# A recurrence pipeline in another order: inverse, state and output work of a chunked scan re-sequenced on PE, VectorE and ScalarE

## The reference

```python
def _wkv_step(S, inp):
    r_t, w_t, k_t, v_t, a_t, b_t = inp
    sa = jnp.einsum('zbhvk,zbhk->zbhv', S, a_t)
    S = S * w_t[..., None, :] + sa[..., :, None] * b_t[..., None, :] + v_t[..., :, None] * k_t[..., None, :]
    return S, jnp.einsum('zbhvk,zbhk->zbhv', S, r_t)

def rwkv_out(y, h, xx, r, k_mod, v, mu, ln_g, ln_b, r_k, g1, g2, wo):
    ...
    y = layernorm(y, ln_g.reshape(RWKV_HEADS, RWKV_HEAD), ln_b.reshape(RWKV_HEADS, RWKV_HEAD), GN_EPS)
    bonus = jnp.einsum('bthk,zbthk->bth', _heads(r) * r_k, _heads(k_mod))
    y = y.astype(r.dtype) + bonus[..., None] * _heads(v)
```

## Time and profile before

| | us |
|---|---|
| median of 3 runs (lowest, highest) | 3682.07 (3679.72, 3685.00) |
| profiled execution, its own time | 3685.94 |
| its span, first to last instruction | 3684.0 |
| granted TensorE clock, mean over the span | 0.863 |
| PE busy, share of the span | 2950.9, 80% |
| VectorE (DVE) busy | 1179.1, 32% |
| ScalarE (ACT) busy | 484.1, 13% |
| GpSimd (POOL) busy | 241.5, 7% |
| the scan, from 2377.5 to 3002.1 of the span | 624.6 |

### The profile page before, as it was taken

One profiled execution on the slowest core, in us unless ns is written; L12 is line 12 of the kernel. 1 busy time (PEld: TensorE's weight loads), 2 busy tenths in 40 slices (PEclk: granted clock), 3 DMA queues, 4 the chain that ended last, 5 costly groups with the idle time before them and its releaser, 6 DMA issues. The chain is left out here.

```text
span 3684.0 us, 58651 instructions
## 1 busy us (share of the span) xinstructions
PE 2950.9 (80%) x25609; PEld 2059.6 (56%) x25609; DVE 1179.1 (32%) x2475; ACT 484.1 (13%) x1017; POOL 241.5 (7%) x230
## 2 busy tenths in 40 slices
PE   6999859999799897487777469788888883878775
PEld 5877625787684553344444224377777862444443
DVE  3562374355115102310000142265565522100002
ACT  1000212100111000100000000143333311000001
POOL 0000000000000000100000000032222201000000
PEclk9999755999699678599898779899999996998997
DMA  6774110577123100699999701000000016999994
GB/s 216 240 222 129 42 63 1 199 243 231 46 74 98 34 23 11 258 384 396 398 395 391 274 31 62 23 3 3 3 3 3 3 47 264 388 392 395 394 392 195
DMA packets 288698, 642.12 MB, mean 174 GB/s; under 512 B 27625, under 2 KB 180761, under 8 KB 254921
## 3 DMA queue, kind: packets, MB, share of 16 engines
q1 hardware_dynamic: 243124, 540.54, 40.1%
q10 hardware_dynamic: 37910, 74.88, 5.6%
q0 software_dynamic: 7424, 23.12, 2.1%
HBM read 611.70 MB, written 26.77 MB: 173 GB/s over the span
## 5 line engine op out<-in xcount | busy, mean ns | idle before, releaser
L1624 PE MATMUL bank<-expert_weights,ex_xt 128*64 128x256 f32 x2688 | 346.5, 417 | 100.3 <-DMA expert_weights<-in_moe_w_up_dram 100.0
L1624 PEld LDWEIGHTS bank<-expert_weights,ex_xt 128*64 128x64 f32 x2688 | 233.1, 151 | 228.0 <-issue 158.0
L444 PE MATMUL bank<-u,weights 128*128 128x272 f32 (+1 forms) x1408 | 318.6, 390 | 14.0 <-DVEq L465 14.0
L444 PEld LDWEIGHTS bank<-u,weights 128*128 128x128 f32 x1408 | 270.7, 192 | 62.0 <-DVEq L465 14.8
L1675 DVE TENSOR_TENSOR ex_hidden<-ex_silu,bank 128x256 f32<-128x256 f32 x64 | 26.9, 421 | 716.1 <-ACT ex_silu L1660 716.1
L1624 PE MATMUL bank<-weights,ex_xt 128*64 128x256 f32 x1408 | 186.7, 426 | 53.0 <-DMA weights<-in_moe_w_up_dram 51.5
L1032 DVE SCALAR_TENSOR_TENSOR ada_acc<-ada_w,cond,ada_acc 128x512 f32 (+1 forms) x336 | 227.5, 744 | 0.0
L515 PE MATMUL bank<-rw_mixed,weights 128*128 128x512 f32 (+2 forms) x448 | 188.5, 582 | 39.7 <-DVEq L523 36.2
L1624 PEld LDWEIGHTS bank<-weights,ex_xt 128*64 128x64 f32 x1408 | 124.2, 154 | 122.1 <-issue 85.9
L515 PE MATMUL bank<-hidden,weights 128*128 128x272 f32 (+1 forms) x704 | 160.8, 392 | 14.9 <-DVEq L523 14.9
L1645 PE MATMUL bank<-expert_weights,ex_hidden_turned 128*64 128x512 f32 x672 | 153.5, 598 | 21.7 <-DVE ex_hidden_turned L1678 21.7
(11 more groups left out here) (503 smaller groups left out, 4311.6 us busy)
## 6 DMA issues: line engine op xcount, KB each, us to landing
expert_weights<-in_moe_w_gate_dram SPq DMA_DIRECT2D x84, 1024.0 KB, 26.1
expert_weights<-in_moe_w_up_dram SPq DMA_DIRECT2D x84, 1024.0 KB, 26.6
expert_weights<-in_moe_w_down_dram SPq DMA_DIRECT2D x84, 1024.0 KB, 26.0
ada_w<-in_ada_w_dram ACTq DMA_DIRECT2D x24, 2048.0 KB, 8.7
weights<-in_moe_w_gate_dram SPq DMA_DIRECT2D x44, 1024.0 KB, 25.4
weights<-in_moe_w_up_dram SPq DMA_DIRECT2D x44, 1024.0 KB, 26.0
weights<-in_moe_w_down_dram SPq DMA_DIRECT2D x44, 1024.0 KB, 25.8
weights<-in_w_gate_dram SPq DMA_DIRECT2D x22, 1024.0 KB, 5.3
```

The costliest lines, as they stand in the source:

```text
L444: last = nc.tensor.matmul(k.bank[b + side * NB][:, 0:N], w[:, f, c * P:(c + 1) * P], rhs[:, f, 0:N], start=(f == DC - 1), stop=(f == 0))
L1624: last = nc.tensor.matmul(half_cols(k.bank[2 + side], t), xt[:, s, f * SLOTS:(f + 1) * SLOTS], w[:, q * 512 + t * 256:q * 512 + t * 256 + ...
```

## The change

Which piece follows which in the three loops is changed, four methods are split so that their parts can stand at different places, and three waits are adapted. No instruction's shape changes and no arithmetic.

- PE: in the tail of a pass the level-5 t of direction 1, and side product 0 of the *next* back half, come ahead of the last xt; the first y sum follows them. The second y sum moves into the next pass, between side products 1 and 2. The next pass begins with n of direction 0; t(1,0) comes ahead of side product 6 and of decay.
- VectorE: `dve_out` is split in three: one instruction after t(1,0), two between rs(0) and xt(1,0), four between update(0) and the decay scan. The exponents are split in one and two instructions. The root moves ahead of xt(4,0). t(5,1) and the second operands move ahead of spread, and `dve_mean` goes to the next pass.
- ScalarE: `act_powers` is split. Square and bonus copy stay at the end of level 3; the first Exp follows update(6), the second x(4,1), the third with the small ones the end of level 4. The copy of side product 0 moves to the tail, the y square and y root to the next pass.
- Unchanged is who empties what: xt of direction 0 stays with VectorE.
- Waits: the first operands wait for `powered` after the second Exp, and only their last instruction (rt) for the rest; side product 0 waits for a new semaphore `bonus_kept`, raised by the bonus copy.

The loops, cut to what the prediction speaks of:

```diff
     def pe(self, pe):
-            if back:
-                self.pe_side(pe, b, 0)
-                self.pe_side(pe, b, 1)
             if front:
                 self.pe_n(pe, c, 0)
             if back:
+                self.pe_side(pe, b, 1)
+                self.pe_y_sum(pe, b - 1, self.q.fix, self.y_squared)
                 self.pe_side(pe, b, 2)
-                self.pe_side(pe, b, 3)
             if front:
                 self.pe_n(pe, c, 1)
             if back:
-                for n in range(4, 7):
+                for n in range(3, 6):
                     self.pe_side(pe, b, n)
+            if front:
+                self.pe_t(pe, c, 1, 0)
+            if back:
+                self.pe_side(pe, b, 6)
             if following:
                 self.pe_decay(pe, p)
-            if front:
-                self.pe_t(pe, c, 1, 0)
...
             if front:
                 self.pe_xt(pe, c, LEVELS - 1, 0)
+                self.pe_t(pe, c, LEVELS - 1, 1)
+                self.pe_side(pe, c, 0)
+                self.pe_xt(pe, c, LEVELS - 1, 1)
             if back:
                 self.pe_y_sum(pe, b, self.q.y, self.y_copied)
-            if front:
-                self.pe_t(pe, c, LEVELS - 1, 1)
-                self.pe_xt(pe, c, LEVELS - 1, 1)
-            if back:
-                self.pe_y_sum(pe, b, self.q.fix, self.y_squared)
+        self.pe_y_sum(pe, DC - 1, self.q.fix, self.y_squared)
...
     def dve(self, dve):
-            if ended:
-                self.dve_out(dve, c - 2)
             if front:
                 self.dve_t(dve, c, 1, 0)
+            if ended:
+                self.dve_out_root(dve, c - 2)
...
                 if back:
                     self.dve_rs(dve, b, i)
+                if ended and level == 1:
+                    self.dve_out_scale(dve, c - 2)
+                if following and level == 4:
+                    self.dve_root(dve, p)
                 if front:
                     self.dve_xt(dve, c, level)
...
                 if back:
                     self.dve_update(dve, b, i)
+                if ended and level == 1:
+                    self.dve_out_gate(dve, c - 2)
                 if following and level == 1:
                     self.dve_decay(dve, p, 0)
...
+                if following and level == 3:
+                    self.dve_exponents(dve, p, 0)
                 if front:
                     self.dve_t(dve, c, level + 1, 0)
...
     def act(self, act):
+                if following and level == 4:
+                    self.act_power(act, p, 0)
                 if back:
                     self.act_rs(act, b, i + 1)
                 if front:
                     self.act_x(act, c, level, 1)
+                if following and level == 4:
+                    self.act_power(act, p, 1)
                 if back:
                     self.act_sa(act, b, i + 1)
...
                 if following and level == 3:
-                    self.act_powers(act, p)
+                    self.act_bonus(act, p)
+            if following:
+                self.act_power(act, p, 2)
...
     def dve_operands(self, dve, c, z):
         if z == 0:
-            dve.wait_ge(self.powered, 2 * c + 2)
+            dve.wait_ge(self.powered, 2 * c + 1)
...
+        if z == 0:
+            dve.wait_ge(self.powered, 2 * c + 2)
         nc.vector.tensor_tensor(rt[:, z, :], q.r[:, c, :], q.G[:, z, :], ALU.mult).then_inc(self.rt_made, 1)
```

More of the change, by code:

```diff
@@ L2467, in dve @@
             b, p = c - 1, c + 1
+            if front:
+                self.dve_n(dve, c, 0)
             if back:
                 self.dve_side(dve, b, 1)
-            if front:
-                self.dve_n(dve, c, 0)
+            if ended:
+                self.dve_mean(dve, c - 2)
             if back:
@@ L2504, in dve @@
                 if following and level == 3:
-                    self.dve_exponents(dve, p)
-                if following and level == 4:
-                    self.dve_root(dve, p)
+                    self.dve_exponents(dve, p, 1)
                 if back:
@@ L2517, in dve @@
                     self.dve_side(dve, b, 8)
-                if following and level == 4:
-                    self.dve_operands(dve, p, 0)
+            if following:
+                self.dve_operands(dve, p, 0)
             if front:
                 self.dve_xt(dve, c, LEVELS - 1)
+                self.dve_t(dve, c, LEVELS - 1, 1)
             if back:
                 self.dve_center(dve, b)
-            if front:
-                self.dve_t(dve, c, LEVELS - 1, 1)
-            if back:
-                self.dve_spread(dve, b)
             if following:
@@ L2668, in dve_mean, with dve_out_root, dve_out_scale @@
             .then_inc(self.m_made, 1)
-    def dve_out(self, dve, b):
+    def dve_out_root(self, dve, b):
+        q, link = self.q, self.link
+        dve.wait_ge(self.y_rooted, 3 * b + 3)
+        link(self.nc.vector.scalar_tensor_tensor(out=q.fix[:, :], in0=q.fix[:, :], scalar=-0.5, in1=q.m[:, :],
+                                                 op0=ALU.mult, op1=ALU.mult))
+    def dve_out_scale(self, dve, b):
         nc, q, link = self.nc, self.q, self.link
-        dve.wait_ge(self.y_rooted, 3 * b + 3)
-        link(nc.vector.scalar_tensor_tensor(out=q.fix[:, :], in0=q.fix[:, :], scalar=-0.5, in1=q.m[:, :],
-                                            op0=ALU.mult, op1=ALU.mult))
         link(nc.vector.scalar_tensor_tensor(out=q.fix[:, :], in0=q.fix[:, :], scalar=1.5, in1=q.root[:, :],
@@ L2691, in act @@
             if back:
-                self.act_side(act, b, 0)
-                for n in range(3, 7):
+                self.act_y_square(act, b - 1)
+                self.act_side(act, b, 3)
+                self.act_y_root(act, b - 1)
+                for n in range(4, 7):
                     self.act_side(act, b, n)
@@ L2713, in act @@
                 if front:
-                    self.act_xt(act, c, level)
+                    self.act_xt(act, c, level, 1)
                 if back and i + 1 < self.LAST:
@@ L2766, in act_powers, with act_power @@
         after(act, self.y_done, p - 2)
-        nc.scalar.activation(q.bonus[p % 3][:, :], k.bank[4][:, 0:SEQ], ACT.Copy)
-        act.wait_ge(self.scaled, p + 1)
-        after(act, self.rt_made, 2 * p)
-        nc.scalar.activation(q.Gp[:, :, :], q.Gp[:, :, :], ACT.Exp, scale=DECAY)
-        nc.scalar.activation(q.lg[:, :, :], q.F[:, :, :], ACT.Exp, scale=-DECAY).then_inc(self.powered, 1)
-        nc.scalar.activation(q.G[:, :, :], q.F[:, :, :], ACT.Exp, scale=DECAY)
-        for z in range(2):
-            after(act, self.s_kept[z], 7 * (p - 2))
-            edge = q.F[:, z, CH - 1::CH] if z == 0 else q.F[:, z, 0::CH]
-            last = nc.scalar.activation(q.pend[p % 3][:, z, :], edge, ACT.Exp, scale=DECAY)
-        last.then_inc(self.powered, 1)
+        nc.scalar.activation(q.bonus[p % 3][:, :], k.bank[4][:, 0:SEQ], ACT.Copy).then_inc(self.bonus_kept, 1)
+    def act_power(self, act, p, part):
+        nc, q = self.nc, self.q
+        if part == 0:
+            act.wait_ge(self.scaled, p + 1)
+            nc.scalar.activation(q.Gp[:, :, :], q.Gp[:, :, :], ACT.Exp, scale=DECAY)
+        elif part == 1:
+            nc.scalar.activation(q.lg[:, :, :], q.F[:, :, :], ACT.Exp, scale=-DECAY).then_inc(self.powered, 1)
+        else:
+            after(act, self.rt_made, 2 * p)
+            nc.scalar.activation(q.G[:, :, :], q.F[:, :, :], ACT.Exp, scale=DECAY)
+            for z in range(2):
+                after(act, self.s_kept[z], 7 * (p - 2))
+                edge = q.F[:, z, CH - 1::CH] if z == 0 else q.F[:, z, 0::CH]
+                last = nc.scalar.activation(q.pend[p % 3][:, z, :], edge, ACT.Exp, scale=DECAY)
+            last.then_inc(self.powered, 1)
     def act_x(self, act, c, level, z):
```

63 lines of the change are left out of this document (39 added, 24 removed).

## The result

The change makes the kernel faster: **3647.94 us** (median of 4 runs, 3646.33 to 3649.49) against 3683.01 (now of 4 runs, 3679.72 to 3685.0), a ratio of 0.9906, 95% interval 0.9888 to 0.9923, so 35 us. The forecast was 3630, its range 3608 to 3660. The profiled execution after took 3646.33 us (span 3644.6), 39.6 less than the one before, and nearly all of that lies in the scan: from the first mask of n to the last y sum it took 592.47 us before and takes 553.18 now.

A forecast was written before the change was run, and what follows sets the result against it. PE was taken to bound the middle levels and to wait at the seam of the passes. Gains over the passes summed to 52.2 us: 3685.9 − 52.2 = 3633.7, as a median 3630, range 3608 to 3660.

The forecast's parts named there:

- L3 and L4: Levels 3 and 4 of a pass: 12.05 to 11.35 us with one exponent moved, 13.96 to 11.3 with rs on time.
- the 1.0 ahead of s(6): In level 4: the root stands ahead of sa(6), 3.0 us behind rs against PE's 2.0, so PE waits 1.0.
- The wait ahead of y(7): In level 4: a 1.04 us Exp holds sa(7) back against 0.93 on PE; already there behind the root, left alone.
- Front: Side products, n, first t and decay: 15.96 to 13.0 us; the y sum's square just hidden, decay's wait 0.9.
- L1: Level 1 of a pass: 10.20 to 15.4 us, with waits of 1.2 and 3.3 and a lower-clock stretch of 1.6.
- Tail: From the last level's xt(5,0) to the first side product: 10.24 to 5.2 us, y sum moved, no lower clock.
- The term: In the tail: PE's wait ahead of xt(5,1), 0.8 us, from VectorE's 4.5 against PE's 3.7.
- The sum: Gains over all passes: 6.3 + 10.2 + 24.8 + 9.2 + 3.6 − 1.9 = 52.2 us.
- the clock did drop in L1: Rival, level 1: the clock does not drop, or gate instructions miss POOL; 3616 to 3622 us, chance 0.17.
- The lower clock did not spread: Rival: PE at the lower clock through level 4, tail and level 1, so slower, 3755 us; chance 0.05.
- More queues: Rival: level 1, level 4, tail and front each hold 0.8 us more in VectorE's queue; 3649 us, chance 0.12.
- table drain: Level 1, ScalarE: the skill page's 1.38 us per table switch would make it 8 us higher; only the range allowed for it.

The follow-up runs named there:

- run 7: Changed kernel with exponents behind rs(5), the Exp in one piece at the end of level 3, and the key root back ahead of sa(7): 3660.18 us.
- run 2: Changed kernel with the four VectorE output gate instructions moved from behind update(0) to behind update(1), at the end of level 1: 3624.17 us.
- run 3: Changed kernel with ScalarE's Sigmoid table load issued right behind the last side copy, ahead of its data: 3631.26 us.
- run 1: Changed kernel with the first operands' wait for y(7) moved to their rt instruction, the only one that needs it: 3627.93 us.
- run 4: Changed kernel with three edits together: later y(7) wait, gate instructions behind update(1), early Sigmoid table load: 3600.35 us.

## Why the forecast was right, and where it missed

- *L3 and L4*: right, to 0.05. The wait of L4 did become the 1.0 ahead of s(6) (0.89 in the bracket, 1.11 start to start), and L4 stands at PEclk 1.00. The wait ahead of y(7) was rightly left alone; run 7 shows that it changed hands.
- *Front*: right where the clock is full, 13.11 for 13.0; no wait for the y sum, and decay's wait 0.79 as before.
- *L1*: right in its terms: sa(0) waits 1.21 (forecast 1.2), sa(1) 3.28 (3.3), the four gate instructions take 3.08 (3.0), and the lower clock comes behind the long wait. How the 3.08 is made up was not foreseen: one of the four waits for GpSimd's product, at 1.53, and not two, and the first takes 0.67. Runs 2 and 3 removed the two waits each by its named cause.
- *Tail: the step that failed.* "The first operands wait for the second exponential only" is wrong; they also wait for y(7), by a line that the change left as it was. The forecast rested on the row ahead of pass 0 in the earlier trace rows, where ScalarE's last Exp is the releaser and no y exists yet. The view of that one line (L2589, the first operand instruction) in the kernel before, with what ended VectorE's idle time ahead of it (us, times), would have said it:

```profile
PE bank L2452: 7.6, 6
  ACT sc_pend L2776: 1.2, 1
```

The term was 0.8 and measures 2.03: 1.2 in each of six tails, 7.4 us (run 1: 8.1 us of idle time). Behind the longer wait the lower clock came in three of the six passes, which the forecast had struck out of tail and front altogether: 1.4 us of the front's 14.54 in the pass shown.
- *The sum*: 52.2 forecast, 39.3 in the scan: 12.9 missing, of which the tail and what it draws in is 11.1 by run 1. The rest lies in the last pass: from the last-but-one centering to the last it takes 0.7 us more than before, where a gain of about 1 was forecast. The median, at 3648 for 3630, missed by 5 us more than the profile: the profiled execution before lay 3.9 above its median, which the forecast took off, and the one after lies 1.6 below its own.
- *The rivals*: the clock did drop in L1. The lower clock did not spread: PE's busy time fell by 15.0. "More queues" gave nearly the time measured, but for another reason: one queue, in the tail, and not a little in four stages. That the time lies in the range is partly luck: its upper end came from that rival and from a table drain that no run shows, not from the wait that was missed.

## What to carry to other kernels

When a wait is taken off an instruction that has several, list all the others at that line and find in the trace which of them ends next; the row that names today's last releaser is not the only one that counts. Look at every instance of the instruction too: here one named ScalarE and six named y(7). Move off-path work behind the instruction that others wait for, on each in-order engine, and look at what the neighbour engine does at the new place. And price a stage by idle time and by busy time apart: the idle times of independent waits added up here to a microsecond, both for the three edits of run 4 and for the change's two halves; the part that came through the clock did so in the first case (12.9 for 11.8) and not in the second (22.3 for 15.0).

## What the runs showed of the hardware

The same wait does not always bring the lower clock. Behind 1.99 us of idle in L4, PEclk is 0.88 over that stage before the change; in run 7 PE waits the same 1.99 there, and the window behind it reads 1.00, the higher level:

```profile
2718.40:2721.80 3.40, 3.39 (x113) 3.40 (x115) 0.88 (x2) 0.54 (x2) 1.27 (x1) 1.00 0.02 5
```

The tail's wait of 1.81 likewise: 0.89 in the front behind it in one pass, 1.00 in the next (both above). Behind 3.06 in L1 it fell in the passes 2 to 6, each time; but in run 3 the clock stayed at 1.00 in one of these five, behind the same 3.06:

```profile
2663.48:2666.89 3.41, 3.41 (x111) 3.41 (x113) 1.48 (x3) 1.25 (x4) 0.00 (x0) 1.00 0.01 2
```

In run 4, where PE's longest wait inside a middle pass is 0.9, it fell in none of the middle passes. What decides between these stays open here.

The VectorE instructions here that read only SBUF pay beside GpSimd's mask products, and not all alike: a 256-wide product of two SBUF operands takes 1.53 us for 0.43, a 128x512 scan instruction 1.60 for 1.22. The masks that read a PSUM bank do not: the one at 2657.41 after the change lies inside GpSimd's product of 2657.24 to 2658.51 and takes 0.69, as the others do. So of two that must run there, here the scan instruction costs VectorE less. GpSimd pays for it in its turn, 1.98 for 1.27 in run 2:

```profile
2664.27 1.98 POOL L2879 TENSOR_TENSOR sc_n<-sc_nt,sc_masks 128x512 f32<-128x512 f32 x1 [0.17 <-PE bank L2159]
```
